# Norms of a transformer block: the sum, root and reciprocal with tokens on partitions, shifts on ScalarE, and three weight tiles side by side where a stage begins

## What is computed

```python
def rms_norm(x, gain):
    y = x * rsqrt(mean(x * x, axis=-1) + 1e-6)
    return y * gain

def swiglu(x, w_gate, w_up, w_down):
    return (silu(x @ w_gate) * (x @ w_up)) @ w_down      # 2816 hidden columns

# first block
x = x + 0.5 * rms_norm(swiglu(rms_norm(x, ffn1_pre), ...), ffn1_post)
u = rms_norm(x, mix_pre)             # sparse attention, delta rule, memory attention
x = x + rms_norm(merged @ w_out, mix_post)
x = x + 0.5 * rms_norm(swiglu(rms_norm(x, ffn2_pre), ...), ffn2_post)

# second block, two layers; shift, scale, gate come from silu(c) @ w_ada + b_ada
for l in range(2):
    h = rms_norm(x, norm[l]) * (1 + scale) + shift       # mixer: convolution and pooling
    x = x + gate * mixer(h)
    h = rms_norm(x, ffn_norm[l]) * (1 + scale2) + shift2 # 32 experts, two per token
    x = x + gate2 * hierarchical_moe(h)
out = rms_norm(x, final)
```

## Time and profile before

| | us |
|---|---|
| three runs | 1970.28, 1971.6, 1979.46 |
| median | 1971.6 |
| span of the profiled execution | 1973.1 |
| TensorE busy in it | 1757.5 |
| VectorE busy | 1494.1 |
| ScalarE busy | 1058.8 |

### The profile page before, as it was taken

How to read it: one execution, slowest core, us unless ns; L and a number is a source line. 1 busy time by engine, 2 the same in 40 slices (tenths; PEclk the granted TensorE clock), 3 DMA queues, 4 the chain that set the end, 5 groups by cost and what they waited for, 6 DMA issues and landing times.

```text
span 1973.1 us, 32962 instructions
## 1 busy us (share of the span) xinstructions
PE 1757.5 (89%) x11920; PEld 1614.3 (82%) x11924; DVE 1494.1 (76%) x2099; ACT 1058.8 (54%) x1449; POOL 3.7 (0%) x9
## 2 busy tenths in 40 slices
PE   7999998999999899967776999999787678999997
PEld 7899998998898899967765788887686667888886
DVE  7788776633547888879965788888799666888886
ACT  4443463233554344333343788888542336888884
POOL 0000000000000000000000000000000000000000
PEclk9999998988999999988987999999799879999998
DMA  9898552123336588833331698989433325898893
GB/s 347 326 309 306 182 173 95 54 99 126 107 118 214 215 308 306 291 103 109 128 118 55 224 342 314 340 318 333 174 129 110 104 97 183 319 339 320 326 331 142
DMA packets 115515, 420.91 MB, mean 213 GB/s; under 512 B 12784, under 2 KB 12800, under 8 KB 115152
## 3 DMA queue, kind: packets, MB, share of 16 engines
q1 hardware_dynamic: 114336, 414.12, 59.8%
q0 software_dynamic: 1072, 5.31, 0.7%
HBM read 416.76 MB, written 2.62 MB: 213 GB/s over the span
## 4 chain that ended last, share of the span: by engine, by line
PE 58%; DVE 25%; ACT 6%; DMA 5%; issue 5%; DVEq 0%; SPq 0%; ACTq 0%
PE work L733 23%; PE acc L733 10%; DVE wlo L1779 9%; DVE yconv L2289 6%; DMA raw<-wstream_d 5%; PE work L1305 5%; PE work L797 4%; ACT whi L1365 4%; PE work L1317 3%; PE work L711 2%; PE work L1251 2%; PE acc L1344 1%; DVE hf L1800 1%; DVE rstd L1790 1%; PE work L782 1%
## 5 line engine op out<-in xcount | busy, mean ns | idle before, releaser
L1779 DVE TENSOR_TENSOR wlo<-raw,whi 128x1024 fp32r<-128x1024 f32 x680 | 816.9, 1223 | 282.2 <-ACT whi L1365 276.8
L1365 ACT ACTIVATE whi<-raw 128x1024 fp32r<-128x1024 f32 x680 | 709.3, 1057 | 536.1 <-PE work L733 385.6
L733 PE MATMUL work<-hhi,whi 128*128 128x256 f32 x1280 | 373.4, 292 | 76.4 <-DVE wlo L1779 47.5
L733 PE MATMUL work<-hlo,whi 128*128 128x256 f32 x1280 | 368.7, 288 | 0.0
L733 PE MATMUL work<-hhi,wlo 128*128 128x256 f32 x1280 | 368.4, 288 | 0.0
L733 PEld LDWEIGHTS work<-hhi,whi 128*128 128x128 f32 x1280 | 250.8, 196 | 84.8 <-DVE wlo L1779 53.3
L733 PEld LDWEIGHTS work<-hlo,whi 128*128 128x128 f32 x1280 | 251.2, 196 | 0.0
L733 PEld LDWEIGHTS work<-hhi,wlo 128*128 128x128 f32 x1280 | 250.9, 196 | 0.0
L2289 DVE SCALAR_TENSOR_TENSOR yconv<-vpad,params,yconv 128x256 f32<-128x256 f32 x240 | 116.1, 484 | 7.1
L1878 DVE SCALAR_TENSOR_TENSOR ada_tiles<-ada_tiles,c_act 128x1024 f32<-128x1024 f32 x96 | 116.4, 1219 | 0.0
L1305 PE MATMUL work<-whi,xg_a 128*128 128x512 f32 x256 | 105.2, 411 | 1.7 <-ACT xg_a L1725 1.7
(11 more groups left out here) (409 smaller groups left out, 3362.9 us busy)
## 6 DMA issues: line engine op xcount, KB each, us to landing
raw<-wstream_d SPq DMA_DIRECT2D x688, 512.0 KB, 4.8
ada_tiles<-ada_d SPq DMA_DIRECT2D x96, 512.0 KB, 5.2
bias_rows_d<-rt POOLq DMA_DIRECT2D x1, 1536.0 KB, 7.5
consts<-consts_d POOLq DMA_DIRECT2D x1, 1063.0 KB, 8.4
xT<-x_d SPq DMA_DIRECT2D x4, 256.0 KB, 4.5
mem_in<-mem_d POOLq DMA_DIRECT2D x1, 1024.0 KB, 6.7
tb<-bias_rows_d POOLq DMA_DIRECT2D x1, 1024.0 KB, 8.5
out_d<-hf SPq DMA_DIRECT2D x4, 256.0 KB, 2.5
```

The lines of the kernel that those rows point to most:

```text
L733: mm = pe.matmul(out, a, b, start=(start and k == 0), stop=(stop and k == n - 1), skip_group_check=skip)
L1365: act.activation(whi[n % AHEAD][:], raw[SPLITS[n] % RAW][:], ACT.Copy).then_inc(s("hi_done"), 1)
L1779: dve.tensor_tensor(wlo[n % AHEAD][:], raw[SPLITS[n] % RAW][:], whi[n % AHEAD][:].bitcast(F32), ALU.subtract).then_inc(s("lo_done"), 1)
```

## The change

It has five parts.

1. **Norms 0, 2 to 7, 9, 10, 12 and 13.** `norm_part` makes the squares the stationary operand and one column of ones the moving one: sixteen products of one column, and the sums of 256 tokens end as two columns with tokens on partitions. ScalarE takes the root of these two columns straight from PSUM, with scale and epsilon in the same instruction; VectorE takes the reciprocal of two columns; two products with the identity (`norm_row`) spread the result over all partitions as a row of 256 in PSUM. `rstd_row` lets VectorE read it there, or copies it for norms 2, 4 and 6. The memory's norm and the layer norms stay as they were.
2. **Table.** `root_table` takes a root of one column ahead of time, at eight places, so that ScalarE's table for the root is loaded there.
3. **Hand-over by chunks.** Scaling, rounding and rest go chunk by chunk. Where there is a shift, ScalarE adds it (`shifted`) instead of VectorE.
4. **Three tiles side by side.** At the start of both swiglus and both mixers `first_tiles` waits for three tiles and takes chunk c of all three before chunk c + 1.
5. **Places.** A swiglu's last weight split, and that of the last output tile of a layer, move behind the root or behind the scaling. Norm 3's sum is spread between the memory's key tiles, its squares behind each evacuation. One more group of twelve tiles of the second swiglu is written out. The first loads are cut: the identity and the gains come ahead of the stream, the rest of the parameters behind tile 3, and `c` behind three tiles. Three preparations of the mixers move behind the first scaling.

```diff
-PEELED = {"ffn1": 2, "ffn2": 0}
+PEELED = {"ffn1": 2, "ffn2": 1}
...
+            sp.dma_start(consts[:, 0:P], consts_d[:, 0:P]).then_inc(s("ident_loaded"), 16)
+            sp.dma_start(params[:, 0:8 * DC], params_d[:, 0:8 * DC]).then_inc(s("gains_loaded"), 16)
...
+            def norm_part(k, j):
+                bank = NORM_BANK[k]
                 if j == 0:
+                    claim([bank], *row_reader[k])
                 pe.wait_ge(s("norm_sq"), NORM_AT[k] + j + 1)
-                for m in range(j * per, (j + 1) * per):
-                    mm = pe.matmul(work[bank][:, 0:T], ones, hf[:, m, :], start=(m == 0), stop=(m == n - 1))
+                for m in (2 * j, 2 * j + 1):
+                    for q in range(QT):
+                        mm = pe.matmul(work[bank][:, q:q + 1], hf[:, m, q * P:(q + 1) * P], ones[:, 0:1],
+                                       start=(m == 0 and q == 0), stop=(m == DC - 1), skip_group_check=True)
...
+            def norm_row(k):
+                pe.wait_ge(s("norm_rstd"), ROWS[k])
+                for q in range(QT):
+                    mm = pe.matmul(work[NORM_BANK[k]][:, q * P:(q + 1) * P], spread(roots_of[:, 2 + q:3 + q], (P,), (0,)),
+                                   ident, start=True, stop=True)
+                mm.then_inc(s("norm_row"), 1)
...
+            def first_tiles(r, banks, part):
+                tiles = [tile_ready(r + n) for n in range(len(banks))]
+                for c in range(DC):
+                    pe.wait_ge(s("h_ready"), DC * H_INDEX[part] + c + 1)
+                    a = slice(c * P, (c + 1) * P)
+                    for bank, (h, l) in zip(banks, tiles):
+                        mm = product(work[bank][:, 0:T], [((h[:, a], l[:, a]), (hhi[:, c, :], hlo[:, c, :]))],
+                                     start=(c == 0), stop=(c == DC - 1))
+                        if c == DC - 1:
+                            mm.then_inc(s("pe_tile"), 1)
...
-            norm_sum(2, 0)
+            norm_sum(2)
+            norm_row(2)
             pe.wait_ge(s("mem_ready"), 4)
             for m in range(4):
                 feature_tile(START["memk"] + m, memhi, memlo, 1 + m % 3)
-            norm_sum(3, 0)
+                if m < 3:
+                    norm_part(3, m)
+                if m == 2:
+                    norm_part(3, 3)
+            norm_row(3)
...
             def roots(k):
...
+                times = 4.0 if k in TIMES_TWO else 1.0
+                act.wait_ge(s("norm_sum"), k + 1)
+                act.activation(roots_of[:, 0:2], work[NORM_BANK[k]][:, 0:2], ACT.Sqrt,
+                               bias=eps[:, 1:2] if k in TIMES_TWO else eps[:, 0:1], scale=times / D
+                               ).then_inc(s("norm_std"), 1)
+            def root_table():
+                act.activation(roots_of[:, 4:5], eps[:, 0:1], ACT.Sqrt)
...
+            def shifted(part, l, at):
+                for c in range(DC):
+                    act.wait_ge(s("scaled"), DC * MODULATED[part] + c + 1)
+                    act.activation(hf[:, c, :], hf[:, c, :], ACT.Identity,
+                                   bias=mod[:, l * 48 + at * DC + c:l * 48 + at * DC + c + 1]).then_inc(s("hf_done"), 1)
+                    if part in H_INDEX:
+                        high_h(part, (c,))
...
             swiglu("ffn1")
+            root_table()
             act.wait_ge(s("mem_ready"), 4)
             squares_ffn(0, START["memk"])
             roots(2)
+            hi(NUMBER[START["memk"] - 1] + AHEAD)
             for m in range(4):
                 r = START["memk"] + m
-                if m == 3:
-                    squares_x(1)
                 hi(NUMBER[r] + AHEAD)
                 evac(r, kmem[:, m, :], 1 + m % 3)
-            roots(3)
+                if m < 3:
+                    squares_x(1, (m,) if m < 2 else (2, 3))
+                if m == 2:
+                    roots(3)
...
+            def rstd_row(k, between=None):
+                dve.wait_ge(s("norm_std"), k + 1)
+                dve.reciprocal(roots_of[:, 2:4], roots_of[:, 0:2]).then_inc(s("norm_rstd"), 1)
+                if between:
+                    between()
+                dve.wait_ge(s("norm_row"), ROWS[k])
+                row_of[0] = work[NORM_BANK[k]][:, 0:T]
+                if k in (2, 4, 6):
+                    own(dve.tensor_copy(rstd[:], row_of[0]))
+                    row_of[0] = rstd[:]
...
+            def normalise(part, src, gain, between=None):
+                for c in range(DC + 1):
+                    if c < DC:
+                        scaled_chunk(c, src, gain).then_inc(s("hf_done"), 1)
                     if between:
+                        between(c)
+                    if c > 0:
+                        rest_chunk(part, c - 1)
+            def modulated(part, src, scale):
+                for c in range(DC + 2):
+                    if c < DC:
+                        scaled_chunk(c, src, scale).then_inc(s("scaled"), 1)
+                    if part in H_INDEX and c > 1:
+                        rest_chunk(part, c - 2)
...
             normalise("ffn1", x_chunk, lambda m: col("ffn1_pre", m),
+                      lambda c: lo({1: 0, 3: 1, 5: 2}[c]) if c in (1, 3, 5) else None)
+            lo(3)
             swiglu("ffn1")
```

More of the change, by code:

```diff
@@ L295 @@
 NORM_AT = [sum(n for j, n in enumerate(NORM_PARTS[:k]) if j != 1) for k in range(len(NORM_PARTS))]
+WIDE = (1, 8, 11)
+NARROW = [k for k in range(8 + 3 * LAYERS) if k not in WIDE]
+VARS = {k: n + 1 for n, k in enumerate(WIDE)}
+ROWS = {k: n + 1 for n, k in enumerate(NARROW)}
+NORM_BANK = {k: 3 if k in (0, 5, 7, 10) else 0 for k in NARROW}
+TIMES_TWO = (2, 6)
+MODULATED = {"mixer0": 0, "experts0": 1, "mixer1": 2, "experts1": 3}
 HF_INDEX = {"ffn1": 0, "mix": 1, "ffn2": 2, "mixer0": 3, "experts0": 4, "mixer1": 5, "experts1": 6}
@@ L617, in load_ada @@
                 sp.dma_start(ada_tiles[:, a % ADA_RING, :], src).then_inc(s(f"ada_loaded{a % ADA_RING}"), 16)
-            load(0)
-            load(1)
+            for r in range(3):
+                load(r)
             sp.dma_start(c_act[:], c_d).then_inc(s("c_loaded"), 16)
-            for r in range(2, RAW):
+            load(3)
+            sp.dma_start(params[:, 8 * DC:NFIRST], params_d[:, 8 * DC:NFIRST]).then_inc(s("params_loaded"), 16)
+            for r in range(4, RAW):
                 load(r)
@@ L1378, in square, with squares_x @@
                 act.activation(flat_hf[:, a], src[:, a], ACT.Square).then_inc(s("norm_sq"), 1)
-            def squares_x(update):
-                for j in range(4):
+            def squares_x(update, pairs=range(4)):
+                for j in pairs:
                     act.wait_ge(s("x_ready"), 4 * (update - 1) + j + 1)
@@ L1660, in _ @@
                     act.wait_ge(s("layer_params"), 16)
-                high_h(f"mixer{l}")
+                shifted(f"mixer{l}", l, 0)
                 for m in range(8):
@@ L1699, in _ @@
                 roots(k + 2)
+                hi(NUMBER[START[f"wout{l}"] + DC - 1] + AHEAD)
+                shifted(f"experts{l}", l, 3)
                 act.wait_ge(s("router_centred"), 2 * l + 1)
@@ L1780, in lo, with variance @@
                                   ALU.subtract).then_inc(s("lo_done"), 1)
-            def variance(k, n, times=1.0, src=None):
+            def variance(k, n, src):
                 dve.wait_ge(s("norm_sum"), k + 1)
-                dve.tensor_scalar(var[:], src if src is not None else work[0][:, 0:T], times ** 2 / n,
-                                  times ** 2 * EPS, ALU.mult, ALU.add).then_inc(s("norm_var"), 1)
+                dve.tensor_scalar(var[:], src, 1.0 / n, EPS, ALU.mult, ALU.add).then_inc(s("norm_var"), 1)
+            row_of = [None]
+            def rstd_row(k, between=None):
[8 more added lines that the diff above has]
+                    row_of[0] = rstd[:]
             def root_done(k):
@@ L1808, in normalise @@
+                return scaled_chunk(2 * j + 1, src, gain)
             def normalise(part, src, gain, between=None):
-                for j in range(5):
-                    if j < 4:
-                        scaled_pair(j, src, gain).then_inc(s("hf_done"), 1)
+                for c in range(DC + 1):
+                    if c < DC:
+                        scaled_chunk(c, src, gain).then_inc(s("hf_done"), 1)
                     if between:
-                        between(j)
-                    if j > 0:
-                        rest_pair(part, j - 1)
@@ L1818, in modulated @@
-            def modulated(part, src, scale, shift):
-                own(scaled_pair(0, src, scale))
-                for j in range(4):
-                    shifted_pair(j, shift)
-                    if j < 3:
-                        ins = scaled_pair(j + 1, src, scale)
-                    if part in H_INDEX and j > 0:
-                        rest_pair(part, j - 1)
-                    if j < 3:
-                        own(ins)
-                if part in H_INDEX:
```

(11 more changed lines are left out.)

206 lines of the change are left out of this document (117 added, 89 removed).

## The result

| | before | after |
|---|---|---|
| median, us (4 runs each) | 1974.88 | 1997.01 |
| lowest to highest | 1970.28 to 1979.46 | 1991.89 to 1997.88 |
| span of the profiled execution | 1973.1 | 1996.2 |
| time of it at the lower clock | 253 | 279 |

A forecast was written before the change was run, and what follows sets the result against it. TensorE, busy 1757.5 of 1973.1 us, was taken as the bound, with VectorE bounding the mixers. The places (9.2 + 12.0 + 5.1 - 1.8 - 7.4 - 1.6 - 1.2) gave +14 on 1971.6: 1985.5 us, range 1967 to 1998.

The forecast's parts named there:

- Opening: Start to first down tile: first product at 21.0, down tile at 40.2, then 1.7 for a cold restart; +9.2 us.
- Memory tiles: First swiglu's end and key tiles: three waits of 2.05 for norm 3's squares, plus low clock; +12.0 us in all.
- the clock: Tiles behind each new sum begin at 1.2 GHz: 2.0 us after a whole norm, 1.7 for a restart, bounds 0 and 3.4.
- second rival: Low clock throughout the memory tiles: each pause costs 3.4, another +8 to +12 there, 1996 us; 12% chance.
- Output product to second swiglu: Norms 4 and 5 to second swiglu's first down tile: tile 0 ends +3.4 later, restart +1.7; +5.1 us.
- table load: Early root table loads: norm 4's path loses 0.6; by the Trainium skill's 2.66 us per switch, the sum would be +17.
- Mixer 0: Second swiglu's end to mixer 0's first glu: glu at 880.1 where it was 881.82; -1.8 us.
- mixer 1: Start of mixer 1: as mixer 0, but with no branch norm ahead that shortens; -1.6 us.
- Experts: Experts' input, twice: shorter chain (-1.7) and fewer VectorE operations start the router 3.7 us earlier each; -7.4 us.
- Final norm: Last norm: its chain goes from 2.7 to 1.5; -1.2 us.
- first rival: The clock goes as before, since one-column sums keep it: 0 in sum, 1971.7 us, no change; 22% chance.
- The third: Full clock where stages begin: tiles out 2.0 us earlier at four places, no restart loss; -13, 1958.6 us; 13% chance.

The follow-up runs named there:

- e2: The changed kernel with one tile in place of three at the start of both swiglus: 1982.16 us, ratio 1.0040 to the kernel before.
- e4: The changed kernel with one tile in place of three at the start of both mixers: 1986.56 us, ratio 1.0062 to the kernel before.
- e9: The kernel of e6 with the changed kernel's one-column sums again: 1971.15 us, ratio 0.9990 to the kernel before.
- e6: The changed kernel with 128-column sums, one tile opening each swiglu, norm 3's sum behind the fourth key tile: 1957.93 us, ratio 0.9923.
- e1: The changed kernel with 128 columns of ones in place of one in the new sums: 1977.82 us, ratio 1.0018 to the kernel before.
- e7: The kernel of e6 with the output products' early root table load moved behind the third weight split: 1958.32 us, ratio 0.9915.

## Why the forecast was right, and where it was short

1. **Opening (+9.2 forecast).** Every landmark up to the first down tile came within 1.1 us: sum's end 11.8 (11.9), first product 21.1 (21.0), idle 5.88 (5.7), down tile 41.3 (40.2). The whole place measured +11.3, since the restart at the low clock cost 2.8 (11.3 less 8.5) and not 1.7.
2. **Memory tiles (+12.0).** The three waits were there, 2.0 us each as worked out, but the place measured +15.4. The failed term is the clock, put at 2.0 for the first tile and 1.3 for each later one. The low stretches were 235.1 to 241.9, 245.3 to 252.1, 255.6 to 259.0 and 262.4 to 269.2, 23.8 us in all, against 3.4 us in this place before. Half of the 20 more is 10 us; the place itself has 9.3 beside the 6.1 of waiting, where the forecast had 5.9 for the clock. This is the second rival's mechanism, at 3.4 of the 8 to 12 more that it asked for (by its own price of 3.4 for each start, 7.7); its 1996 met the total because other places made up the rest, which is luck. The Trainium skill (TensorE: Matmul & The Clock Gate, "HAM oscillation") names such a return of the low clock for a kernel with few output rows that waits 3 to 5 us for a DMA before each batch; the trace shows the return here with waits of 2.0 us for ScalarE.
3. **Output product to second swiglu (+5.1).** Measured +5.1, from +24.6 to +29.7, but two misses cancel. The table load ahead of the first split lets an output tile wait (0.77 us at 646.46, and 0.71 at 1058.99 in layer 0), which I had put at nothing, and the first product comes 1.2 later than forecast. In return the tiles' start at the low clock, put at 2.0, cost about half a us: products start 0.21 apart at first and 0.12 apart from the sixth on. TensorE in the changed kernel:

```profile
677.65 0.55 PE L767 MATMUL work<-hhi,whi 128*128 128x256 f32 x1
...
678.64 0.37 PE L767 MATMUL work<-hlo,whi 128*128 128x256 f32 x1
678.85 0.28 PE L767 MATMUL work<-hhi,wlo 128*128 128x256 f32 x1
678.97 0.28 PE L767 MATMUL work<-hhi,whi 128*128 128x256 f32 x1
```

4. **Mixer 0 (-1.8) and mixer 1 (-1.6).** Measured -1.4 and -1.2 at their glus.
5. **Experts (-3.7 each).** From the sum's end to the router it is 3.5 us shorter in both. From glu to router the net is -2.4 and -3.2, since the output tile's wait above counts against it here as well.
6. **Final norm (-1.2).** From the experts' end to the end it is 15.03 us in place of 12.79, so +2.2: wrong in sign. I had taken the sum at the full clock; it ran wholly at the lower one, and the row product too. TensorE in the changed kernel:

```profile
1981.39 6.82 PE L728 MATMUL work<-ones,hf 128*128 128x1 f32 x32
...
1988.77 1.22 PE L742 MATMUL work<-consts,roots_of 128*128 128x128 f32 x4 [0.55 <-DVE roots_of L1890]
```

It need not do so: e2 and e4, with the same thin sum, ran it in 3.79 and 3.70.

The misses add up: 2.1 (opening), 3.4 (memory tiles), 0.8 (mixers), 1.8 (experts), 3.4 (final norm), less 2.8 that came back in stages whose operations the edits leave alone (2.1 between memory tiles and output product, 1.4 in layer 0's experts, less 0.7 in layer 1's): 8.7, against 23.1 - 14.3 = 8.8.

The large ones have one term in common, the clock. I priced it place by place, a short stretch behind each new sum; e9 against e6 shows that thin sums alone bring 39 us more at the lower clock (252 and 213, the medians over all runs of the two) and 13 us of time. In e1 beside the changed kernel it is 62 less (217 and 279) and 19 us. By these two pairs an estimate is that a microsecond more at the lower clock costs this kernel a third of one. With e9 the first rival, that the clock goes as before, fell. The third, full clock where stages begin, came half true in the second swiglu (item 3) and gained nothing, as the idle of 5.80 stood behind it. Of the table load, the Trainium skill (ScalarE: Activation LUTs, "What ACT_TABLE_LOAD costs") has 1.28 us and a drain of 1.38, 2.66 in all. The trace has the 1.28, and no drain: the root starts 0.02 behind the load (643.47 to 644.77 in the changed kernel). e7 shows that moving it gains nothing.

What stays open: 3 of e2's 15 us lie outside the two swiglus (7.1 and 4.8), as most of e4's saving lies outside the mixers. That this comes only from the moments at which the clock falls was argued, not shown. Nor do the runs show what in a thin sum lets the clock fall; they compare 1 column with 128 and nothing between.

## What to carry to other kernels

A reduction on TensorE should keep its moving operand wide when that costs nothing: 128 equal columns took about the time of one (3.8 us and 3.7 for a sum) and saved 13 us of 1971. Tiles that share their end also share their release, so with a ring of four buffers and three tiles side by side the split of the fifth tile comes late, and so does all that is queued behind it (5.9 and 5.8 us of waiting, 2.0 and 0.7 before). Between tiles put the small operation that the next product needs ahead of the weight split and the evacuation; and take a change like this one apart, since without its three losing places the rest is 0.8% faster than the kernel before.

## What was not expected of the hardware

32 fp32 records with a stationary tile of 128 x 128 take 3.7 to 3.8 us with one moving column (e4, e2) and 3.8 to 3.9 with 128 columns (e6, e1), at a nearly full clock; but only behind the wide ones was the next product at the full clock (0.71 for four records against 1.22). Begun at the low clock, behind 3.56 us of waiting, the wide sum took 5.39, as the clock rose within it, and the thin one 6.96. And two kernels can differ by 4 us in a stage that they have in common.
